# The cached-attention stage of a hybrid decoder step: sequences as separate steps, or one stream of 153 turns

## The reference, cut to what matters

```python
def diff_attend(q, q_pos, k, v, k_pos, lam):
    s = jnp.einsum('bqhcd,bkhcd->bhcqk', q, k).astype(jnp.float32) * (QK_HEAD ** -0.5)
    s = jnp.where(k_pos[None, :] <= q_pos[:, None], s, -jnp.inf)
    p = jax.nn.softmax(s, axis=-1)
    a = p[:, :, 0] - lam * p[:, :, 1]
    return jnp.einsum('bhqk,bkhd->bqhd', a, v.astype(jnp.float32))
...
        # prompt: 8 blocks of 128 queries, 4 heads, keys 0..1023
        # samples: 4 queries, 4 heads, keys from the pages and 4 new ones
        k_past = cache_k[l, page_table].reshape(bs, past, N_HEADS, 2, QK_HEAD)
        v_past = cache_v[l, page_table].reshape(bs, past, N_HEADS, V_HEAD)
```

## Time and profile before

| | before |
|---|---|
| median of 3 runs | 2258.97 us (2254.36 to 2262.54) |
| the profiled execution: its time | 2256.54 us |
| its span, first to last instruction | 2254.7 us |
| TensorE, VectorE, ScalarE, GpSimd busy, share of the span | 80%, 47%, 22%, 14% |
| mean granted TensorE clock, of full speed | 0.896 |
| moved by DMA | 404.41 MB, of it 270.55 MB on the gathers' queue |
| stage 3 | about 425 to 1222 us |

### The profile page before, as it was taken

The page is one execution under the profiler, slowest core; times in us unless marked ns, Lnnn a source line. Parts: engine busy times, 40 slices in busy tenths (PEclk is TensorE's granted clock), DMA queues, the critical chain, the costliest instruction groups (busy, mean ns, idle before and its releaser), DMA issues.

```text
span 2254.7 us, 40461 instructions
## 1 busy us (share of the span) xinstructions
PE 1795.3 (80%) x17492; PEld 1469.9 (65%) x17492; DVE 1056.0 (47%) x1532; ACT 488.1 (22%) x831; POOL 319.0 (14%) x287
## 2 busy tenths in 40 slices
PE   5799999566665766666665994999999999799991
PEld 2277899545554554555454893777777777799991
DVE  2324121476776775767662557112111111465567
ACT  0211111012212122121221104111112110344441
POOL 0000000123232422324322005200000000000003
PEclk8899999677987988879885996999999999899996
DMA  9701123577988989879877310121121121621112
GB/s 310 279 24 51 38 82 123 193 253 300 409 335 322 414 334 414 329 324 414 346 324 299 113 43 13 57 72 59 56 93 56 59 72 37 226 84 40 47 36 96
DMA packets 133284, 404.41 MB, mean 179 GB/s; under 512 B 12153, under 2 KB 76665, under 8 KB 100338
## 3 DMA queue, kind: packets, MB, share of 16 engines
q0 software_dynamic: 37392, 270.55, 29.7%
q1 hardware_dynamic: 87426, 127.52, 16.7%
q10 hardware_dynamic: 8320, 4.19, 0.7%
HBM read 377.79 MB, written 24.51 MB: 178 GB/s over the span
## 4 chain that ended last, share of the span: by engine, by line
PE 63%; DVE 18%; DMA 12%; issue 5%; ACT 1%; DVEq 0%; POOL 0%; SPq 0%; ACTq 0%
PE psum L746 27%; PE psum L995 11%; PE psum L754 10%; DMA k_ring<-cache_k,page_idx 7%; DVE k_turned L1433 6%; DMA ada_w<-w_ada 3%; PE psum L845 2%; PE psum L855 2%; DVE p_t L427 2%; PE psum L729 2%; PE psum L825 1%; DVE x_lo L1278 1%; DMA v_ring<-cache_v,page_idx 1%; PE psum L874 1%; DVE soft L1384 1%
## 5 line engine op out<-in xcount | busy, mean ns | idle before, releaser
L1433 DVE STREAM_TRANSPOSE k_turned<-k_ring 128x2048 f32<-128x2048 f32 x128 | 295.5, 2308 | 7.2 <-DMA k_ring<-cache_k,page_idx 6.9
L746 PE MATMUL psum<-x_hi,w_hi 128*128 128x512 f32 x896 | 281.3, 395 | 0.0
L746 PE MATMUL psum<-x_lo,w_hi 128*128 128x512 f32 x896 | 277.2, 391 | 0.0
L845 PE MATMUL psum<-k_turned,q_blocks 128*32 128x128 f32 x4096 | 157.6, 301 | 150.0 <-DVE k_turned L1433 149.8
L746 PE MATMUL psum<-x_hi,w_lo 128*128 128x512 f32 x896 | 275.9, 389 | 0.0
L1297 DVE TENSOR_TENSOR w_lo<-w_raw,w_hi 128x2048 fp32r<-128x2048 f32 x37 | 86.9, 2350 | 361.9 <-ACT w_hi L1053 352.6
L845 PEld LDWEIGHTS psum<-k_turned,q_blocks 128*32 128x32 f32 x4096 | 117.4, 119 | 205.4 <-issue 153.8
L995 PE MATMUL psum<-d_hi,h_hi 128*128 128x256 f32 x704 | 203.1, 288 | 12.0 <-DVE d_lo L1647 10.7
L995 PE MATMUL psum<-d_lo,h_hi 128*128 128x256 f32 x704 | 200.3, 285 | 0.0
L995 PE MATMUL psum<-d_hi,h_lo 128*128 128x256 f32 x704 | 200.2, 284 | 0.0
L746 PEld LDWEIGHTS psum<-x_hi,w_hi 128*128 128x128 f32 x896 | 165.6, 188 | 44.8 <-issue 5.3
(11 more groups left out here) (228 smaller groups left out, 2503.9 us busy)
## 6 DMA issues: line engine op xcount, KB each, us to landing
ada_w<-w_ada SPq DMA_DIRECT2D x12, 2048.0 KB, 9.0
w_raw<-w_in SPq DMA_DIRECT2D x12, 1024.0 KB, 5.3
w_raw<-w_gate SPq DMA_DIRECT2D x11, 1024.0 KB, 5.4
w_raw<-w_up SPq DMA_DIRECT2D x11, 1024.0 KB, 6.2
h_store<-h_out SPq DMA_DIRECT2D x11, 1024.0 KB, 7.8
h_all<-h_store SPq DMA_DIRECT2D x11, 1024.0 KB, 8.2
d_raw<-w_down SPq DMA_DIRECT2D x44, 256.0 KB, 3.1
x_rows<-x_prompt SPq DMA_DIRECT2D x2, 2048.0 KB, 17.9
```

Source lines behind the costliest of these rows:

```text
L746: last = mm(psum[:, 2 * ft + c, 0:CH], w[:, s, k, ft * P:(ft + 1) * P], x[:, k, c * CH:(c + 1) * CH], start=k == 0 and j == 0, stop=k == K ...
L845: last = mm(psum[QUAD * h:QUAD * (h + 1), g % 2, 0:GP * QUAD], q_blocks[:, h, d, :], k_turned[:, g % 2, :, h * HD + d * QUAD:h * HD + (d + ...
L1433: v.transpose(k_turned[:, g % 2].rearrange("p j n -> p (j n)"), k_ring[:, g].rearrange("p j n -> p (j n)")).then_inc(k_free, 1)
```

## The change

The steps become one stream of 153 turns, written out in Python without a loop of the hardware. In turn n stands key group n (n under 128) and value group n - 23, so values follow their keys by a sequence and seven turns, across the borders of sequences. The softmax of a sequence is cut into pieces which stand in turns 0 to 7 of the next 16, beside groups and tiles; it has two `s_rows`, two `q_blocks`, one PSUM bank for turned exponentials, used four times, and the regrouping is done for a quarter of the scores at a time. VectorE turns key group n + 1 in turn n, in place in `k_ring`; `k_turned` is gone, and a key buffer is given back once its group is scored. The prompt starts at turn 6: per head two turns bring its keys and queries, then 4 turns to a tile, tiles 0 to 7 in order; head 3 ends at turn 141. Later heads' rows are fetched by SyncE's queue in place of ScalarE's.

```diff
-        TILES = ([i for i in range(NT) if i % 4 in (0, 3)], [i for i in range(NT) if i % 4 in (1, 2)])
+        LAG = STEP + 7
+        SLOTS = NK + LAG + 2
+        HEAD0, HEAD_SLOTS = 6, 2 + 4 * z.NT
+        TILES = list(range(NT))
+        ACC, MISC, TURNED, ROWS, OUT = 2, 3, 4, 5, 7
+        def dense_at(n):
+            if not HEAD0 <= n < HEAD0 + H * HEAD_SLOTS:
+                return None, None, None
+            h, r = (n - HEAD0) // HEAD_SLOTS, (n - HEAD0) % HEAD_SLOTS
+            if r < 2:
+                return h, None, r
+            return h, h * NT + (r - 2) // 4, (r - 2) % 4
...
-        def regroup(copy, j):
+        def regroup(copy, j, r):
+            got = psum[QUAD * j:QUAD * (j + 1), TURNED, :].rearrange("p (g h a q) -> p g h a q", h=H, a=4, q=8)
             to = p_t[:].rearrange("p (g j) (h q) -> p g j h q", j=4, q=8)
             for a in range(4):
-                last = copy(to[QUAD * a:QUAD * (a + 1), :, j], got[:, :, :, a, :])
+                last = copy(to[QUAD * a:QUAD * (a + 1), 4 * r:4 * (r + 1), j], got[:, :, :, a, :])
...
+            for n in range(NK + LAG):        # GpSimd
+                if n < NK:
+                    if n >= RK:
+                        pool.wait_ge(scored, n - RK + 1)
+                    gather(k_pages, k_ring[:, n % RK], k_in[n % RK], n)
+                if n >= LAG:
+                    m = n - LAG
+                    if m >= RV:
+                        pool.wait_ge(v_used, m - RV + 1)
+                    gather(v_pages, v_ring[:, m % RV], v_in[m % RV], m)
...
+            def slot(n):                     # TensorE
+                b, s = n // STEP, n % STEP
+                if n < NK:
+                    if s == 0:
+                        new_keys(b)
+                    key_group(n)
+                if LAG <= n < NK + LAG:
+                    value_group(n - LAG)
+                if 1 <= b <= B:
+                    if s == 1:
+                        turn_max(b - 1)
+                    elif s == 2:
+                        max_to_rows(b - 1)
+                    elif 4 <= s < 4 + REVS:
+                        turn_p(b - 1, s - 4)
+                    if s == 5:
+                        fold_sums(b - 1)
+                if s == 8 and b >= 2:
+                    by_query(b - 2)
+            for n in range(SLOTS):           # TensorE: tiles ahead of the slot
+                h, u, q = dense_at(n)
...
+                elif q == 0:
+                    if u % NT:
+                        weigh_rows(u - 1)
+                    scores(u, 0)
+                elif q == 1:
+                    scores(u, 1)
+                elif q == 3:
+                    turn_rows(u)
+                slot(n)
...
+            def turn_keys(n):                # VectorE
+                dve.wait_ge(k_in[n % RK], 16 * (n // RK + 1))
+                group = k_ring[:, n % RK].rearrange("p j n -> p (j n)")
+                v.transpose(group, group).then_inc(k_turned, 1)
+            def slot(n):
+                b, s = n // STEP, n % STEP
+                if n + 1 < NK:
+                    turn_keys(n + 1)
+                if s == 0 and 1 <= b <= B:
+                    maximum(b - 1)
+                if s == 0 and b < B:
+                    new_scores(b)
+                if b < B:
+                    if s in (4, 8, 12):
+                        turn_maxima(b, s // 4 - 1)
+                    elif s == 10 and b + 1 < B:
+                        queries(b + 1)
+                if 1 <= b <= B:
+                    if s == 1:
+                        spread_max(b - 1)
+                    elif s == 2:
+                        negative_max(b - 1)
+                    elif 4 <= s < 4 + REVS:
+                        keep_p(b - 1, s - 4)
+                    if s == 5:
+                        keep_sums(b - 1)
+                if s == 6:
+                    if b >= 2:
+                        scale_output(b - 2)
+                    if 1 <= b <= B:
+                        keep_scale(b - 1)
+            for n in range(SLOTS):           # VectorE: take_rows, slot, then the tile
...
+                slot(n)
+                if u is not None and q == 0:
+                    maxima(u, 0)
+                elif u is not None and q == 1:
+                    maxima(u, 1)
+                elif u is not None and q == 2:
+                    combine(u)
```

More of the change, by code:

```diff
@@ L443, in load_pages, with gather @@
         def load_pages(pool):
[L446 to L458, removed]
+            def gather(rows, to, landed, n):
+                pool.indirect_dma_start(to.rearrange("p s d -> p (s d)"), None, rows,
+                                        bass.IndirectOffsetOnAxis(page_idx[:, n:n + 1], 0)).then_inc(landed, 16)
+            for n in range(NK + LAG):
[8 more added lines that the diff above has]
+                    gather(v_pages, v_ring[:, m % RV], v_in[m % RV], m)
         def fetch_head(eng, h):
@@ L912, in _ @@
-            step(0, 0, 0, first=True)
-            with pe.Fori(0, H - 1) as i:
-                step(2 * i + 1, i, 1)
-                step(2 * i + 2, i + 1, 0)
-            step(B - 1, H - 1, 1)
-            softmax(B - 1)
-            for r in range(REVS):
-                for g in range(RING):
-                    value_group(B - 1, r, g, (r, g) == (REVS - 1, RING - 1))
-            by_query(B - 1)
+                        last = mm(psum[QUAD * h:QUAD * (h + 1), ACC, 0:P], p_t[:, g * GP + j, :],
+                                  v_ring[:, m % RV, j, h * HD:(h + 1) * HD], start=False, stop=g == STEP - 1 and j == GP - 1)
@@ L1116, in step @@
-            def step(b, h, half, first=False):
-                if not first:
-                    softmax(b - 1)
-                for r in range(REVS):
-                    n, i = b * REVS + r, TILES[half][r]
-                    for g in range(RING):
-                        if g == 3:
-                            keep_turned(n, i)
-                        take_scores(b, r, g)
-                        if g < 2:
-                            exps(n, i, g)
-                if not first:
-                    keep_output(b - 1)
@@ L1130, in _, with keep_p @@
-            step(0, 0, 0, first=True)
-            with act.Fori(0, H - 1) as i:
-                act.wait_ge(rows_turned, i + 1)
-                fetch_head(act, i + 1)
-                step(2 * i + 1, i, 1)
-                step(2 * i + 2, i + 1, 0)
-            step(B - 1, H - 1, 1)
-            softmax(B - 1)
-            keep_output(B - 1)
+            def keep_p(e, r):
+                act.wait_ge(p_turned, REVS * e + r + 1)
+                if e:
+                    act.wait_ge(v_used, STEP * (e - 1) + 4 * (r + 1))
+                for j in range(2):
+                    last = regroup(copy, j, r)
+                last.then_inc(p_by_act, 1)
@@ L1467, in step @@
-            def step(b, h, half, first=False):
-                if first:
-                    head_start(h)
-                else:
-                    softmax(b - 1, h if half == 0 else None)
-                queries(b)
-                for r in range(REVS):
-                    n, i = b * REVS + r, TILES[half][r]
-                    for g in range(RING):
-                        turn_keys(b, r, g)
-                        if g == 1 and r:
-                            link(turn_maxima(b, r - 1))
-                        if g < 2:
-                            maxima(n, i, g)
-                        elif g == 2:
-                            combine(n, i)
-                        else:
-                            take_rows(h, n, i)
-                if not first:
-                    scale_output(b - 1)
```

413 lines of the change are left out of this document (231 added, 182 removed).

## The result

The changed kernel takes 2291.35 us (median of 4 runs, 2286.13 to 2292.69); the kernel before took 2256.66 beside it (4 runs, 2250.68 to 2262.54). The ratio is 1.0149, with a 95% interval of 1.0116 to 1.0182: slower by some 35 us. The prediction said 45 us faster. The sign is wrong, and the time lies outside the range.

What follows compares the result with a forecast made beforehand. Stage 3 was taken as transfer-bound inside a step and starved at borders and ends. Its end: 439 + 82 + 559 + 75 + 22 = 1177 against 1221.8, 45 us less, so 2213 us for the kernel; range 2168 to 2254.

Steps and rivals of the forecast that it cites:

- turns 20 to 127: Middle of stage 3's stream: transfers need 541 us, VectorE's program 574; 559 taken, between 541 and 590.
- together 4.6 assumed: Turns 20 to 127: softmax pieces' mutual waits and ScalarE's exponentials ahead of a tile's, 4.6 us per 16 turns, 0 to 10.
- the forecast's smoothing: Turns 20 to 127: rings smooth a few microseconds where lighter and heavier tiles change; 559 us taken instead of 574.
- Turns 128 to 141: Values alone beside head 3's last tiles and sequence 7's softmax: 75 us, bounds 55 and 90.
- Rival D: Lockstep waits of 8 to 10 us per sequence bring the middle to 605 us: no change, 2259 us; chance 0.03.
- A: Transfers set the pace throughout; middle 541 us, tail 60, start 78, kernel 2176 us; chance 0.20.
- Rival B: Key ring too short, buffers held until scored: 5.9 us per turn, middle 637, kernel 2291 us; chance 0.10.
- C: The ends eat the gain: 110 us for the tail, 92 for the start, kernel 2258 us; chance 0.12.
- The start: Turns 0 to 19, from the first turning at 439 to pass 23 at 521: 82 us, bounds 74 to 92.
- the last stretch: Turns 142 to 152, nine value groups alone to the stage's end: 22 us.
- The loop's end: Two VectorE idle stretches where the loop goes round, one 5.26 us, vanish when written out; nothing put on instruction fetching.
- The transfers' limit: Stage 3's gathers reckoned at 418 GB/s, from the trace, against the skill's about 358; a pair takes 5.02 us.

Runs made afterwards that it cites:

- tile_first: Changed kernel with each turn's tile maxima, combine and exponentials put ahead of the softmax piece on VectorE and ScalarE: 2198.21 us, 0.9763 of the kernel before.
- decode_alone: Changed kernel without the prompt's attention (no tiles or heads, its rows a constant), all gathers and rings kept: 2143.87 us, one run.
- best_spread: Changed kernel with tile ahead of pieces, prompt from turn 0, light tiles ending the stream, regrouping spread over eight turns: 2172.37 us, 0.9631 of the kernel before.

## Why the prediction was wrong

**The step that failed** is that of turns 20 to 127, and in it one term: "together 4.6 assumed (0 if the engines stand a turn apart, 10 if each costs its round trip)" for the softmax pieces' lockstep. The stretch took 76 us more than forecast, 11.3 for each of its 6.75 sequences, so with the forecast's smoothing from 574 to 559 kept the term is 15.9. Without smoothing, 635.1 us are 94.1 for 16 turns against 80.4 for the rest of the sum, and it is 13.7. Both are beyond the upper bound; counted from the transfers' pace, 80.3 for 16 turns, it is 14.5. The list of VectorE's instructions was right and their costs nearly so; wrong was how they stand to each other. I summed VectorE's program and added waits as if each chain ran by itself. The place to look was the order within a turn: on VectorE the copies ahead of the maxima, on TensorE the tile's scores ahead of the turned exponentials. The diff shows both. Followed through one turn they give a closed chain, which in the timeline above is scores 3.8, groups 2.3, turning 0.7, copies 2.4, maxima 1.5 and exponentials 1.1: 11.8 us for tile 7, end to end. Rows of before had sizes for such a sum (scores 1.88, copies 8 x 274 ns; with 1.88 for the scores it comes to some 10); it wasn't made. Tile_first, which moves nothing but that order, gives 93 us back, and its 564 us in turns 20 to 127 lie 5 above the forecast's 559.

**A term that was hit by luck.** Turns 128 to 141 took 74.3 us for 75. Nothing was put there for a round trip, yet the last sequence's four pieces stand in them behind second scores and `turn_rows` as in the middle, and tile_first takes 54. So the tiles and pieces by themselves were priced some 20 us too high, and the round trip filled that up. That tile_first's 2198 us lie under the predicted 2213 is mostly these 20 us.

**Rival D** named this mechanism (lockstep waits in each sequence), with a chance of 0.03 and a price of 8 to 10 us, where 13.7 to 15.9 came. No row was named against it, as one was against A and B, so 0.03 had nothing to stand on.

**Rival B's** 2291 us is the time measured, by coincidence. Its mechanism was that keys land too late for a ring held until scoring. After has turnings waiting 44.0 us for keys in all, its median landing is 10.6 us (15.2 before), and decode_alone sustains 5.05 us a turn with the same ring. Buffers did come free late, but as a result of the long turns: GpSimd's gather at 835.43 had waited 10.50 us for a key group that stood behind the scores.

**Rivals A and C.** A's floor is nearly reached, but only by other kernels (558 us in best_spread, 564 in tile_first; 541 predicted for A). C is refuted: the ends took 76.7, 74.3 and 26.0 us, against the 92 and 110 that it needed. The start was 5 us shorter than predicted, the last stretch 4 longer.

**The terms that held.** The first turning starts at 443.4, not 439. VectorE is busy 461.95 us in turns 20 to 127, 68.4 per 16 turns; 69.8 was predicted. Its groups by shape for the turnings and the regrouping, with the columns of the earlier trace rows:

```profile
L1491 DVE STREAM_TRANSPOSE k_ring<-k_ring 128x2048 f32<-128x2048 f32 x128 | 294.6, 2304 | 44.3 <-DMA k_ring<-cache_k,page_idx 44.0
...
L441 DVE COPY p_t<-psum 32x128 f32<-32x128 f32 x256 | 74.5, 291 | 80.5 <-PE psum L920 77.2
```

For the copies 8.8 us a sequence were predicted and 9.3 measured (74.5/8); turning in place costs what it did before.

**The loop's end.** The two idle stretches on no semaphore, 10.7 us together on VectorE before, one of them the 5.26 of the earlier trace rows, are gone: VectorE's longest there in stage 3 is now 0.3 us. TensorE's matmuls show 1.8 at most. GpSimd has one of 7.2 before a gather of keys, not explained here. Putting nothing on fetching the straight program was right within these few microseconds.

**The transfers' limit.** Tile_first moves 401 GB/s on average over 564 us, best_spread 407 over 555. The Trainium skill, "SBUF — State Buffer", section "A bandwidth-pool intuition that's wrong (but worth ruling out)", gives some 358 GB/s for this path; these traces disagree over half a millisecond at a time, so measuring by 418 was right.

**What is settled and what is open.** Shown: the order of pieces and tile costs 93 us (68 with copies spread); spreading the pieces gives 40 or 15 by the same table; the deal of tiles within a head costs nothing; the key ring isn't the cause. Open: how the 6 us per sequence by which tile_first's turns 4 to 7 (26.1) still exceed four pairs of transfers (20.1) divide between copies and other waits; how the 40 us that spreading gives in the changed kernel divide between fewer copies in a turn and turnings that stand in other turns than second scores and `turn_rows`; and what more key buffers would give with the value buffers kept, which wasn't tried.

## What to carry to other kernels

When a serial piece is cut up and woven into a pipeline of engines that work in order, list for one turn each engine's instructions in order and draw who waits for whom; if the new piece and the old work pass through the same engines in opposite order of precedence, two short chains become one long one, whatever the busy times say. Put first on each engine what another engine waits for soonest, and spread the pieces so that no turn's own work exceeds the pace that the transfers set. A predicted time that is hit, of the whole or of one stretch, proves no mechanism: look for its wait in the trace.

## What the runs showed that was not expected

A regrouping copy out of PSUM to 32 partitions takes 691 ns for 512 columns and 291 ns for 128, so a quarter of the columns costs 0.42 of the time. Two points give 158 ns fixed and 1.04 ns a column: cutting the regrouping in four added some 30 us of VectorE's time over the kernel (74.5 for 44.2).

The granted TensorE clock of turns 20 to 127 is 0.81 in the changed kernel and 0.87 in tile_first, for the same matmuls: TensorE is then busy 66% and 71% of the stretch, and its busy time is 418.87 against 399.35 us. The timeline above shows how that enters the chain. The four products of the scores at 830.21, after 6.30 us of idling, took 3.78 us; the same four for the first component at 819.55, with no idling before them, took 1.88. The busy times of the two stretches:

```profile
819.50:821.40 1.90, 1.90 (x10) 0.67 (x10) 1.84 (x8) 0.54 (x3) 0.00 (x0) 1.00 0.99 388
...
830.20:834.00 3.80, 3.79 (x8) 1.25 (x12) 0.94 (x1) 0.00 (x0) 0.00 (x0) 0.50 0.06 26
```

The granted clock is 1.00 in the first and 0.50 in the second, the higher and the lower of TensorE's two levels (2.4 and 1.2 GHz). So 1.9 of this chain's 11.8 us come from the clock that was granted after the wait. How much of the 93 us this is over all turns wasn't separated.
